# The first prompt tile's output projection moved from the merge block to the end of the sample attention's block

## Chip, cores and metric

The kernel runs on one core of a Trainium2 chip (trn2), in float32. The metric is the device time of one execution in microseconds (us). "Runs" below are executions without the profiler; a profile is one further execution that the hardware profiler recorded.

## What is computed

One layer of a decoder for 512 prompt tokens and 64 sample tokens (8 sequences of 8), width 1024. Cut to what matters here:

```
x = x_prompt (512 rows), x_sample (64 rows)
sh1, sc1, ga1, sh2, sc2, ga2 = split(silu(c) @ w_ada + b_ada)
h   = rms_norm(x, g_pre_mix) * (1 + sc1) + sh1
z   = h @ w_in                                  # q, k, v, u, s
a   = rms_norm(attend(q, k, v), g_subln)        # prompt: causal; sample: 2048 cached keys + its own
s   = gelu(u) * (spatial gating of layer_norm(gelu(zs)))
mix = concat([a, s], -1) @ w_out                # the projection of this change: 1024 x 1024
x   = x + ga1 * rms_norm(mix, g_post_mix)
h2  = rms_norm(x, g_pre_ffn) * (1 + sc2) + sh2
y   = top-1 of 4 groups, top-2 of 4 experts (SwiGLU) on h2
out = x + ga2 * rms_norm(y, g_post_ffn)
```

## The kernel before

The kernel is written engine by engine, with semaphores set by hand. An engine works through its own list in order; nothing is reordered by a scheduler. The program is a row of blocks: condition, project and `attend_prompt` in one; `attend_sample` in a block of its own; then `merge` and `experts`; then the rest. At a block's end each engine drains and all meet (line 930 for the sample block). After the sample block `forget` (from line 243) clears semaphores and has all engines meet once more. Then each jumps to its part of `merge`.

The 576 tokens are five tiles, t = 0 to 3 with 128 prompt tokens each and t = 4 with the 64 sample tokens. `attend_prompt` has written the prompt tiles' rows of `mix` before the sample block begins, so tile 0's projection needs nothing of the sample attention.

**The sample block's tail.** `values(f)` (lines 1172 and 1175) is the last TensorE work for a sequence. ScalarE copies half of its result (line 1011), VectorE adds, masks and reduces (1097, 1100, 1105), and GpSimd stores it (966), waits for the last two stores, and drains. SyncE has loaded `w_out` in two halves of 2 MB into ring slots 0 and 1 in this block (line 946).

**The merge block.** For tile t TensorE turns the rows of `mix` round with 8 transposes (`mix_tr`, line 1573), ScalarE and VectorE each copy half of them to `mixT` (`evac_mix`, 1323 and 1389), and TensorE runs 16 matmuls of 128x512 (line 1611; each has two rows in the trace, so a tile has 32). ScalarE squares the result and sums it (1359), GpSimd takes the power -1/2 (737, 738), VectorE scales it and adds x (1435, 1436: `x1_done`). ScalarE squares x1 (1365) and VectorE makes h2 (1441, 1442). While TensorE projects tile t it waits, before its second half, for `x1_done` of tile t-1.

What stands first on two engines matters here. ScalarE's list in `merge` begins with `evac_mix(0)`, and then issues 21 loads on its own queue: `g_post_mix`, `g_pre_ffn` and three rows of the modulation (these five raise `mod_in`), x of tile 0 among them (1336 to 1341), x of the other tiles (1343), eight pieces of the sample output (1345) and three more (1348). Then comes the loop over tiles, the square first. VectorE's part begins so:

```
dve.wait_ge(self.table_in, 64)
link(dve.memset(self.logits, 0.0))
evac_mix(0)
dve.wait_ge(mod_in, 16 * 5)
modulation(0, P)
for t in range(NT):
    ...
    if t + 1 < NT:
        evac_mix(t + 1)
```

`modulation` (lines 1408, 1409) multiplies the loaded rows. So VectorE's copy for tile 1 stands behind the wait for `mod_in`, and ScalarE's copy for tile 1 stands behind its loads and the square of tile 0. SyncE's expert weights (line 1211) wait for `mod_in` and all x.

Of the kernel before, what the change touches and what calls it, by code (L numbers as in the profile page):

```python
# [18 lines left out]
ACT = mybir.ActivationFunctionType  # L19
# [4 lines left out]
P = 128  # L24
D = 1024
KC = D // P
# [39 lines left out]
def rows(t):  # L66

    return P if t < 4 else NS
# [117 lines left out]
class Program:  # L186
    def __init__(self, nc, a, o, where, ncst, ctx):
# [17 lines left out]
        self.mod_outs = self.lasting("mod_outs")  # L205
        self.mod = nc.dram_tensor("mod_rows", (NS + 1, 6 * D), F32).ap()
# [697 lines left out]
    def attend_sample(self):  # L904
# [25 lines left out]
        with nc.Block() as block:  # L930
# [50 lines left out]
            def _(act):  # L981
# [34 lines left out]
                looped(act, step)  # L1016

            @block.vector
            def _(dve):
# [87 lines left out]
                looped(dve, step)  # L1107

# [95 lines left out]


# [9 lines left out]
    def merge(self, block):  # L1215
# [3 lines left out]
        (o_in, ss_ready, ss_power, mix_ready, mod_in, tr_done, ev_a, ev_d, proj_done, sq1, rs1, x1_done,  # L1219
# [3 lines left out]
                 "o_in", "ss_ready", "ss_power", "mix_ready", "mod_in", "tr", "ev_a", "ev_d", "proj",  # L1223
# [13 lines left out]
        mixT = [L.at(L.HT + D * i, D).rearrange("p (k t) -> p k t", k=KC) for i in range(2)]  # L1237
# [46 lines left out]
        def proj_bank(t, c):  # L1284

            return 3 if c == 1 - t % 2 else (4 if c else 2)
# [30 lines left out]
        def _(act):  # L1317
            def evac_mix(t):
                n = rows(t)
                act.wait_ge(tr_done, t + 1)  # L1320
                if t >= 2:
                    act.wait_ge(proj_done, t - 1)
                act.activation(mixT[t % 2][:, 0:4, 0:n],
                               PS[:, 0, :].rearrange("p (k t) -> p k t", k=4)[:, :, 0:n], ACT.Copy).then_inc(ev_a, 1)

# [8 lines left out]
            evac_mix(0)  # L1334
# [15 lines left out]
            for t in range(NT):  # L1350
                n = rows(t)
                if t < 4:
                    act.wait_ge(proj_done, t + 1)
                else:
                    act.wait_ge(summed, 2)
                if t >= 2:
                    act.wait_ge(h2_tr, t - 1)
                    act.wait_ge(h2_out2[t % 2], 16 * (t // 2))
                act.activation(hv[t % 2][0:n], proj(t, n), ACT.Square, accum_out=ss1[0:n, t:t + 1]).then_inc(sq1, 1)
                if t >= 1:  # L1360
                    evac_h2(t - 1)
                if t + 1 < NT:
                    evac_mix(t + 1)
                act.wait_ge(x1_done, t + 1)
                act.activation(hv[t % 2][0:n], self.x1[0:n, t, :], ACT.Square,
                               accum_out=ss2[0:n, t:t + 1]).then_inc(sq2, 1)
                act.wait_ge(h2_done, t + 1)
                act.dma_start(self.h2[P * t:P * t + n, :], hv[t % 2][0:n]).then_inc(h2_out2[t % 2], 16)
# [12 lines left out]
        def _(dve):  # L1381
            link = chain(dve, dchain)

            def evac_mix(t):
                n = rows(t)
                dve.wait_ge(tr_done, t + 1)
                if t >= 2:
                    dve.wait_ge(proj_done, t - 1)
                dve.tensor_copy(mixT[t % 2][:, 4:8, 0:n],  # L1389
                                PS[:, 1, :].rearrange("p (k t) -> p k t", k=4)[:, :, 0:n]).then_inc(ev_d, 1)  # L1390
# [22 lines left out]
            evac_mix(0)  # L1413
            dve.wait_ge(mod_in, 16 * 5)
            modulation(0, P)
            for t in range(NT):
# [13 lines left out]
                if t + 1 < NT:  # L1430
                    evac_mix(t + 1)
# [132 lines left out]
        def _(pe):  # L1564
            def mix_tr(t):
                n = rows(t)
                if t >= 1:
                    pe.wait_ge(ev_a, t)
                    pe.wait_ge(ev_d, t)
                if t == 4:  # L1570
                    pe.wait_ge(mix_ready, 1)
                for k in range(KC):
                    last = pe.transpose(PS[:, k // 4, (k % 4) * P:(k % 4) * P + n], L.mix[0:n, t, k::KC],
                                        L.cst("ident", n)[:, 0:n])
                last.then_inc(tr_done, 1)
# [22 lines left out]
            mix_tr(0)  # L1598
            for t in range(NT):
                n = rows(t)  # L1600
                pe.wait_ge(ev_a, t + 1)
                pe.wait_ge(ev_d, t + 1)
                for i, c in enumerate((t % 2, 1 - t % 2)):
                    if t == 0:
                        pe.wait_ge(self.ring_full[W_OUT[c]], 16 * STATIC_USES[W_OUT[c]] + 16)
                    if t >= 2 - i:
                        pe.wait_ge(x1_done, t - 1 + i)
                    w = L.ring[W_OUT[c]].rearrange("p (k n) -> p k n", k=KC)
                    if t < 4:
                        for k in range(KC):  # L1610
                            last = pe.matmul(PS[:, proj_bank(t, c), :], mixT[t % 2][:, k, :], w[:, k, :],  # L1611
                                             start=k == 0, stop=k == KC - 1)
# [9 lines left out]
                if t >= 1:  # L1622
                    h2_tr_of(t - 1)
                if t + 1 < NT:
                    mix_tr(t + 1)
                if t >= 1:
                    logits_of(t - 1)
# [440 lines left out]
```

## Time and profile before

| | before |
|---|---|
| median of 3 runs | 1033.86 us (1033.08 to 1035.77) |
| the profiled execution's own time | 1031.1 us |
| its span in the trace | 1029.3 us |
| mean granted TensorE clock, share of full | 0.907 |
| TensorE (PE) busy | 825.5 us, 80% of the span |
| VectorE (DVE) busy | 345.0 us, 34% |
| ScalarE (ACT) busy | 210.0 us, 20% |
| GpSimd (POOL) busy | 121.7 us, 12% |
| DMA | 257.52 MB, mean 250 GB/s |

The span is that of one execution; its own time is 1.8 us longer, and 2.8 us under the median of the runs. A share of busy time is a mean over stages with different limits, so what counts for this change is read from the stretch between 545 and 600 us, where the sample block ends and the merge begins.

### The profile page before, as it was taken

The numbers are of one execution on the slowest core, as the hardware profiler recorded it, in microseconds if no ns is written. First come the engines' busy times: TensorE is split into PE (matmuls) and PEld (weight loads), VectorE is DVE, ScalarE is ACT, GpSimd is POOL, SyncE is SP. The second block draws the span as 40 slices with busy tenths as digits, with TensorE's granted clock in tenths as the row PEclk, the third lists the DMA queues.
The fourth block names the chain that finished last, engine by engine and source line by source line (L and its number), as shares of the span: only waits on it lengthen the run. The fifth ranks groups of instructions, "written<-read, shape, count | busy, mean of one in ns | idle before, by whom it ended". The sixth has DMA issues, their size and how long they took to land. (4 is left out here: it accounts for less than half of the span.)

```text
span 1029.3 us, 12324 instructions
## 1 busy us (share of the span) xinstructions
PE 825.5 (80%) x4656; PEld 429.3 (42%) x4656; DVE 345.0 (34%) x799; ACT 210.0 (20%) x437; POOL 121.7 (12%) x204
## 2 busy tenths in 40 slices
PE   0329999999788869899875999249998999999940
PEld 0024444444455545665642455234443444444410
DVE  0143630021578755555530354530110111001017
ACT  0200100100556423433420121100110111111113
POOL 1310100000400011322210010010000000000024
PEclk9959999999679889999986999559999999999975
DMA  8959412382892017999972951514789899999835
GB/s 258 253 165 348 169 56 77 118 305 65 316 401 65 1 61 309 389 414 425 378 285 113 337 223 61 205 62 173 273 327 411 354 388 399 377 415 379 346 115 192
DMA packets 49293, 257.52 MB, mean 250 GB/s; under 512 B 5704, under 2 KB 6952, under 8 KB 38880
## 3 DMA queue, kind: packets, MB, share of 16 engines
q1 hardware_dynamic: 30224, 151.54, 38.7%
q0 software_dynamic: 10672, 86.72, 22.1%
q10 hardware_dynamic: 8352, 18.66, 5.7%
q8 instruction: 29, 0.48, 0.2%
q14 instruction: 16, 0.13, 0.0%
HBM read 234.07 MB, written 22.83 MB: 250 GB/s over the span
## 5 line engine op out<-in xcount | busy, mean ns | idle before, releaser
L695 PE MATMUL ps<-sb 128*128 128x512 f32 x320 | 142.8, 601 | 0.0
L1820 PE MATMUL ps<-sb 128*128 128x512 f32 (+1 forms) x256 | 114.2, 599 | 0.0
L695 PEld LDWEIGHTS ps<-sb 128*128 128x128 f32 x320 | 60.3, 192 | 73.7 <-issue 73.3
L1122 PE MATMUL ps<-sb 128*128 128x128 f32 x512 | 64.9, 281 | 18.4 <-ACT sb L991 9.3
L1774 DVE TENSOR_TENSOR sb<-sb,ps 128x512 f32<-128x512 f32 (+1 forms) x16 | 10.9, 684 | 190.9 <-PE ps L1820 127.6
L1122 PEld LDWEIGHTS ps<-sb 128*128 128x128 f32 x512 | 56.7, 143 | 31.7 <-issue 17.4
L1812 PE MATMUL ps<-sb 128*128 128x512 f32 x144 | 66.8, 618 | 1.0 <-ACT sb L1738 0.8
L1833 PE MATMUL ps<-sb 128*128 128x512 f32 x144 | 63.5, 594 | 0.0
L1611 PE MATMUL ps<-sb 128*128 128x512 f32 x128 | 58.8, 619 | 1.9 <-DVE sb L1389 0.9
L1817 PE MATMUL ps<-sb 128*64 128x512 f32 x112 | 50.9, 608 | 7.5 <-DMA sb<-in_w_up 7.5
L1820 PEld LDWEIGHTS ps<-sb 128*128 128x128 f32 (+1 forms) x256 | 42.5, 168 | 34.4 <-issue 34.4
L879 PE MATMUL ps<-sb 128*128 128x128 f32 (+3 forms) x128 | 53.2, 556 | 3.2 <-ACT sb L792 3.2
L442 PE MATMUL ps<-sb 128*9 128x512 f32 x192 | 22.6, 624 | 39.6 <-DMA sb<-in_w_ada 39.6
L1038 DVE COPY sb<-ps 128x512 f32<-128x512 f32 x64 | 41.2, 685 | 21.0 <-PE ps L1122 21.0
L805 ACT ACTIVATE sb<-sb 128x128 f32<-128x128 f32 (+3 forms) x64 | 35.4, 554 | 41.9 <-DVE sb L859 41.9
L1812 PEld LDWEIGHTS ps<-sb 128*128 128x128 f32 x144 | 27.7, 198 | 33.7 <-issue 31.8
L991 ACT ACTIVATE sb<-ps 128x512 f32<-128x512 f32 x64 | 34.8, 595 | 32.3 <-PE ps L1122 32.0
L1833 PEld LDWEIGHTS ps<-sb 128*128 128x128 f32 x144 | 26.7, 190 | 31.0 <-issue 30.9
L1611 PEld LDWEIGHTS ps<-sb 128*128 128x128 f32 x128 | 25.1, 199 | 32.9 <-issue 30.4
L1781 DVE COPY sb<-ps 128x512 f32<-128x512 f32 (+1 forms) x16 | 11.1, 692 | 77.6 <-PE ps L1833 54.5
L1172 PE MATMUL ps<-sb 128*32 128x256 f32 x512 | 32.2, 404 | 5.8 <-DMA sb<-in_cache_v,ints 4.7
L1135 PE MATMUL ps<-sb 128*32 128x512 f32 (+1 forms) x320 | 36.6, 530 | 0.0
(254 smaller groups left out, 984.2 us busy)
## 6 DMA issues: line engine op xcount, KB each, us to landing
sb<-in_w_gate SPq DMA_DIRECT2D x16, 2048.0 KB, 12.5
sb<-in_w_up SPq DMA_DIRECT2D x16, 2048.0 KB, 16.9
sb<-in_w_down SPq DMA_DIRECT2D x16, 2048.0 KB, 8.4
sb<-in_w_ada SPq DMA_DIRECT2D x12, 2048.0 KB, 12.8
sb<-in_w_in SPq DMA_DIRECT2D x5, 2048.0 KB, 16.6
y_rows<-sb POOLq DMA_DIRECT2D x1, 5120.0 KB, 36.8
y_rows<-sb SPq DMA_DIRECT2D x9, 512.0 KB, 8.8
sb<-in_x_prompt ACTq DMA_DIRECT2D x8, 512.0 KB, 11.9
```

Of the source, the lines that this page charges most:

```text
L695: last = pe.matmul(PS[:, n % 4, :], L.hT[:, k, t * P:t * P + P], w[:, k, :], start=k == 0, stop=k == KC - 1)
L805: act.activation(pb[n % 3][j][:, 0:w], pb[n % 3][j][:, 0:w], ACT.Exp, bias=nm[:, q:q + 1], accum_out=sums[:, q:q + 1]).then_inc(exp_done, 1)
L879: pe.matmul(PS[:, 2 * (n % 2) + j, 0:P * (i + 1)], qz[i % 2][:, h // 2, 2 * (h % 2) + j, :], L.kT[:, h // 2, 0:P * (i + 1)], start=True, s ...
L991: act.activation(kt[ch % 2][:, h, :], PS[:, h, :], ACT.Copy).then_inc(kt_act, 1)
L1038: dve.tensor_copy(kt[ch % 2][:, h, :], PS[:, h, :]).then_inc(kt_dve, 1)
L1122: last = pe.transpose(PS[:, h, P * g:P * g + P], kp[:, 4 * (ch % 2) + g, P * h:P * h + P], L.cst("ident"))
L1135: last = pe.matmul(bank[32 * h:32 * h + 32, 0:512 if ch < 4 else NS], qst[par][:, h, :], rhs, start=True, stop=True)
L1611: last = pe.matmul(PS[:, proj_bank(t, c), :], mixT[t % 2][:, k, :], w[:, k, :], start=k == 0, stop=k == KC - 1)
L1812: last = pe.matmul(PS[:, 0, :], x[:, k, :], w_gate[:, k, :], start=k == 0, stop=k == KC - 1)
L1817: last = pe.matmul(PS[n:P, 0, :], x[:, k, :], w_gate[:, k, :], start=k == 0, stop=k == KC - 1)
L1820: last = pe.matmul(PS[0:n, 1, :], x[:, k, :], w_up[:, k, :], start=k == 0, stop=k == KC - 1)
L1833: last = pe.matmul(PS[:, 5 + c, :], hT[:, k, :], w[:, k, 512 * c:512 * c + 512], start=k == 0, stop=k == FC - 1)
```

## The change

Tile 0's transposes, its two copies and its 16 matmuls are taken out of `merge` and put behind the last `values` of the sample block, on the same three engines. The bodies become methods of the program (`mix_transpose`, `mix_evac_act`, `mix_evac_dve`, `mix_half`), and four semaphores outlive the block. In `merge`, TensorE begins with tile 1's transposes. The banks, the buffers, the weights and the arithmetic stay the same. The method bodies that the diff removes from `merge` are cut here.

```diff
@@ -1014,6 +1016,7 @@
                         act.activation(S[par], S[par], ACT.Exp, bias=nm[:, par:par + 1],
                                        accum_out=sums[:, par:par + 1]).then_inc(exp_done, 1)
                 looped(act, step)
+                self.mix_evac_act(act, 0)
 
             @block.vector
             def _(dve):
@@ -1105,6 +1108,7 @@
                         dve.tensor_reduce(om[1 - par], osum.rearrange("p g d -> p d g"), AX, ALU.add
                                           ).then_inc(o_ready, 1)
                 looped(dve, step)
+                self.mix_evac_dve(dve, 0)
 
             @block.tensor
             def _(pe):
@@ -1202,6 +1206,60 @@
                         values(f)
                 looped(pe, step)
 
+                pe.wait_ge(kt_act, 2 * 4 * SB)
+                pe.wait_ge(kt_dve, 2 * 4 * SB)
+                self.mix_transpose(pe, 0)
+                pe.wait_ge(self.mix_ev_a, 1)
+                pe.wait_ge(self.mix_ev_d, 1)
+                for c in range(2):
+                    pe.wait_ge(self.ring_full[W_OUT[c]], 16 * STATIC_USES[W_OUT[c]] + 16)
+                    last = self.mix_half(pe, 0, c)
+                last.then_inc(self.proj_done, 1)
+
+
+    def mix_buffers(self):
+        L = self.L
+        return [L.at(L.HT + D * i, D).rearrange("p (k t) -> p k t", k=KC) for i in range(2)]
+
+    def mix_transpose(self, pe, t):
+
+        n = rows(t)
+        for k in range(KC):
+            last = pe.transpose(self.PS[:, k // 4, (k % 4) * P:(k % 4) * P + n], self.L.mix[0:n, t, k::KC],
+                                self.L.cst("ident", n)[:, 0:n])
+        last.then_inc(self.mix_tr, 1)
+
+    def mix_evac_act(self, act, t):
+
+        n = rows(t)
+        act.wait_ge(self.mix_tr, t + 1)
+        if t >= 2:
+            act.wait_ge(self.proj_done, t - 1)
+        act.activation(self.mix_buffers()[t % 2][:, 0:4, 0:n],
+                       self.PS[:, 0, :].rearrange("p (k t) -> p k t", k=4)[:, :, 0:n], ACT.Copy
+                       ).then_inc(self.mix_ev_a, 1)
+
+    def mix_evac_dve(self, dve, t):
+
+        n = rows(t)
+        dve.wait_ge(self.mix_tr, t + 1)
+        if t >= 2:
+            dve.wait_ge(self.proj_done, t - 1)
+        dve.tensor_copy(self.mix_buffers()[t % 2][:, 4:8, 0:n],
+                        self.PS[:, 1, :].rearrange("p (k t) -> p k t", k=4)[:, :, 0:n]).then_inc(self.mix_ev_d, 1)
+
+    def proj_bank(self, t, c):
+
+        return 3 if c == 1 - t % 2 else (4 if c else 2)
+
+    def mix_half(self, pe, t, c):
+
+
+        w = self.L.ring[W_OUT[c]].rearrange("p (k n) -> p k n", k=KC)
+        for k in range(KC):
+            last = pe.matmul(self.PS[:, self.proj_bank(t, c), :], self.mix_buffers()[t % 2][:, k, :], w[:, k, :],
+                             start=k == 0, stop=k == KC - 1)
+        return last
 
     def load_expert(self, sp, e, par, kind):
 
@@ -1331,7 +1380,6 @@
                 act.activation(h2T[t % 2][:, 0:4, 0:m],
                                PS[:, 5, :].rearrange("p (k t) -> p k t", k=4)[:, :, 0:m], ACT.Copy).then_inc(h2_ev, 1)
 
-            evac_mix(0)
             row_of = lambda c: self.mod[NS, c * D:(c + 1) * D].partition_broadcast(P)
             act.dma_start(g_post, a["g_post_mix"].partition_broadcast(P)).then_inc(mod_in, 16)
             act.dma_start(mod[0], row_of(2)).then_inc(mod_in, 16)
@@ -1410,7 +1450,6 @@
 
             dve.wait_ge(self.table_in, 64)
             link(dve.memset(self.logits, 0.0))
-            evac_mix(0)
             dve.wait_ge(mod_in, 16 * 5)
             modulation(0, P)
             for t in range(NT):
@@ -1428,7 +1467,7 @@
                 if t >= 1:
                     evac_h2(t - 1)
                 if t + 1 < NT:
-                    evac_mix(t + 1)
+                    self.mix_evac_dve(dve, t + 1)
                 dve.wait_ge(rs1, t + 1)
                 dve.wait_ge(x_in[t], 16)
 
@@ -1563,16 +1602,11 @@
         @block.tensor
         def _(pe):
             def mix_tr(t):
-                n = rows(t)
-                if t >= 1:
-                    pe.wait_ge(ev_a, t)
-                    pe.wait_ge(ev_d, t)
+                pe.wait_ge(ev_a, t)
+                pe.wait_ge(ev_d, t)
                 if t == 4:
                     pe.wait_ge(mix_ready, 1)
-                for k in range(KC):
-                    last = pe.transpose(PS[:, k // 4, (k % 4) * P:(k % 4) * P + n], L.mix[0:n, t, k::KC],
-                                        L.cst("ident", n)[:, 0:n])
-                last.then_inc(tr_done, 1)
+                self.mix_transpose(pe, t)
 
             def h2_tr_of(t):
                 n = rows(t)
@@ -1595,23 +1629,18 @@
                                          self.w_r[:, k, :], start=k == 0, stop=k == KC - 1)
                 last.then_inc(log_done, 1)
 
-            mix_tr(0)
-            for t in range(NT):
-                n = rows(t)
+            mix_tr(1)
+            for t in range(1, NT):
                 pe.wait_ge(ev_a, t + 1)
                 pe.wait_ge(ev_d, t + 1)
                 for i, c in enumerate((t % 2, 1 - t % 2)):
-                    if t == 0:
-                        pe.wait_ge(self.ring_full[W_OUT[c]], 16 * STATIC_USES[W_OUT[c]] + 16)
                     if t >= 2 - i:
                         pe.wait_ge(x1_done, t - 1 + i)
-                    w = L.ring[W_OUT[c]].rearrange("p (k n) -> p k n", k=KC)
                     if t < 4:
-                        for k in range(KC):
-                            last = pe.matmul(PS[:, proj_bank(t, c), :], mixT[t % 2][:, k, :], w[:, k, :],
-                                             start=k == 0, stop=k == KC - 1)
+                        last = self.mix_half(pe, t, c)
                     else:
 
+                        w = L.ring[W_OUT[c]].rearrange("p (k n) -> p k n", k=KC)
                         for k in range(KC // 2):
                             for c0, kk in ((0, k), (NS, k + KC // 2)):
                                 last = pe.matmul(PS[c0:c0 + NS, proj_bank(t, c), :], mixT[t % 2][:, kk, 0:NS],
```

What this makes of the engines' lists is below. "x16" counts instructions alike in a row; the line numbers are those of each program (1228, 1238, 1248 and 1260 are the new methods' lines, in the order transposes, ScalarE's copy, VectorE's copy, matmuls).

TensorE around the end of the sample block (the two branches are the block's end and the jump to `merge`), before:

```order
L1172 MATMUL ps<-sb 32x256 x32
L1175 MATMUL ps<-sb 32x256 x2
L930 UNCONDITIONAL_BRANCH
L1563 UNCONDITIONAL_BRANCH
L1573 MATMUL ps<-sb 128x128 x8
L1611 MATMUL ps<-sb 128x512 x16
L1573 MATMUL ps<-sb 128x128 x8
L1611 MATMUL ps<-sb 128x512 x16
L1584 MATMUL ps<-sb 128x128 x8
```

The same place with the change:

```order
L1176 MATMUL ps<-sb 32x256 x32
L1179 MATMUL ps<-sb 32x256 x2
L1228 MATMUL ps<-sb 128x128 x8
L1260 MATMUL ps<-sb 128x512 x16
L932 UNCONDITIONAL_BRANCH
L1602 UNCONDITIONAL_BRANCH
L1228 MATMUL ps<-sb 128x128 x8
L1260 MATMUL ps<-sb 128x512 x16
L1618 MATMUL ps<-sb 128x128 x8
```

One group of 8 transposes and 16 matmuls has moved ahead of the two branches; tile 1's group is now the first of the merge.

VectorE at the same place, from the last reduction of the sample output to tile 0's x1, before:

```order
L1105 TENSOR_REDUCE sb<-sb 64x64
L930 UNCONDITIONAL_BRANCH
L1380 UNCONDITIONAL_BRANCH
L1412 MEMSET sb 128x100
L1389 COPY sb<-ps 128x512
L1408 TENSOR_TENSOR sb<-sb 128x1024
L1409 SCALAR_TENSOR_TENSOR sb<-sb 128x1024
L1389 COPY sb<-ps 128x512
L1435 SCALAR_TENSOR_TENSOR sb<-ps,sb 128x1024
```

With the change:

```order
L1108 TENSOR_REDUCE sb<-sb 64x64
L1248 COPY sb<-ps 128x512
L932 UNCONDITIONAL_BRANCH
L1428 UNCONDITIONAL_BRANCH
L1452 MEMSET sb 128x100
L1448 TENSOR_TENSOR sb<-sb 128x1024
L1449 SCALAR_TENSOR_TENSOR sb<-sb 128x1024
L1248 COPY sb<-ps 128x512
L1474 SCALAR_TENSOR_TENSOR sb<-ps,sb 128x1024
```

Tile 0's copy has moved ahead of the branches; tile 1's copy still stands behind the two operations of `modulation`.

ScalarE from its jump into the merge to tile 1's copy, with the change (before, tile 0's copy, `L1323 ACTIVATE`, stood between the branch and the first load):

```order
L1373 UNCONDITIONAL_BRANCH
L1384 DMA sb<-in_g_post_mix 128x1024
L1385 DMA sb<-mod_rows 128x1024
L1386 DMA sb<-in_x_prompt 128x1024
L1387 DMA sb<-in_g_pre_ffn 128x1024
L1388 DMA sb<-mod_rows 128x1024
L1389 DMA sb<-mod_rows 128x1024
L1391 DMA sb<-in_x_prompt 128x1024 x3
L1391 DMA sb<-in_x_sample 64x1024
L1393 DMA sb<-o_sample 8x8x64 x8
L1396 DMA sb<-mod_rows 64x1024 x3
L1407 ACTIVATE sb<-ps 128x1024
```

The loads are now the first thing in the merge's list; the square of tile 0 (line 1407) and tile 1's copy stand behind all of them, as they did.

## Rows read from the trace of the kernel before

**Rows 1.** The page's first part: busy time (share of the span) and instructions.

```profile
PE   825.5 (80%) x4656; PEld 429.3 (42%) x4656; DVE 345.0 (34%) x799; ACT 210.0 (20%) x437; POOL 121.7 (12%) x204
```

**Rows 2.** Timeline, TensorE, 545 to 600 us: start, duration, work [idle before <-releaser].

```profile
546.91 3.04 PE L1172 MATMUL ps<-sb 128*32 128x256 f32 x32 [2.31 <-DMA sb<-in_cache_v,ints]
549.87 1.07 PE L1175 MATMUL ps<-sb 64*32 64x256 f32 x4
559.54 1.94 PE L1573 MATMUL ps<-sb 128*128 128x128 f32 x8 [8.60 <-PEq L243]
562.38 16.79 PE L1611 MATMUL ps<-sb 128*128 128x512 f32 x32 [0.91 <-ACT sb L1323]
579.01 1.04 PE L1573 MATMUL ps<-sb 128*128 128x128 f32 x8
581.00 13.97 PE L1611 MATMUL ps<-sb 128*128 128x512 f32 x32 [0.95 <-DVE sb L1389]
```

**Rows 3.** One line's instructions, 930 (block end), then 243: count, duration ns, start.

```profile
L930 PEldq DRAIN  x1: 3448/3448/3448, 547.5 to 547.5; - x1
L930 POOLq DRAIN  x1: 2832/2832/2832, 555.4 to 555.4; - x1
L243 PEldq EVENT_SEMAPHORE  x1: 51/51/51, 559.4 to 559.4; - x1
```

**Rows 4.** Timeline, VectorE, from 552 to 583 us.

```profile
552.30 0.58 DVE L1105 TENSOR_REDUCE sb<-sb 64x64 f32<-64x256 f32 x1
561.59 0.69 DVE L1389 COPY sb<-ps 128x512 f32<-128x512 f32 x1 [1.86 <-PE ps L1573]
...
573.40 1.23 DVE L1408 TENSOR_TENSOR sb<-sb 128x1024 f32<-128x1024 f32 x1 [11.11 <-DMA sb<-mod_rows]
574.54 1.22 DVE L1409 SCALAR_TENSOR_TENSOR sb<-sb 128x1024 f32<-128x1024 f32 x1
...
581.30 1.28 DVE L1435 SCALAR_TENSOR_TENSOR sb<-ps,sb 128x1024 f32<-128x1024 f32 x1 [0.45 <-POOL sb L738]
582.62 1.23 DVE L1436 TENSOR_TENSOR sb<-sb 128x1024 f32<-128x1024 f32 x1
```

**Rows 5.** Timeline, ScalarE and its queue (ACTq), from 561 to 581 us.

```profile
561.52 0.35 ACTq L1336 DMA_DIRECT2D sb<-in_g_post_mix  x1
...
573.21 1.77 ACTq L1348 DMA_DIRECT2D sb<-mod_rows  x3
579.21 1.02 ACT L1359 ACTIVATE sb<-ps 128x1024 f32<-128x1024 f32 x1 [17.10 <-PE ps L1611]
580.22 0.59 ACT L1323 ACTIVATE sb<-ps 128x512 f32<-128x512 f32 x1
```

**Rows 6.** Windows: stretch, its length, busy (x count) of each engine, PEclk, DMA share, GB/s.

```profile
551.00:554.00 3.00, 0.00 (x0) 0.00 (x0) 1.41 (x3) 0.37 (x1) 0.53 (x1) 1.00 0.00 0
562.30:566.00 3.70, 3.62 (x5) 1.58 (x6) 0.00 (x0) 0.00 (x0) 0.00 (x0) 0.50 0.76 249
566.00:570.00 4.00, 4.00 (x9) 1.70 (x7) 0.00 (x0) 0.00 (x0) 0.00 (x0) 0.74 0.98 353
586.00:600.00 14.00, 14.00 (x73) 8.09 (x72) 6.36 (x7) 2.24 (x5) 0.74 (x2) 1.00 1.01 427
373.90:377.00 3.10, 3.10 (x15) 3.10 (x16) 1.62 (x5) 1.19 (x2) 0.00 (x0) 0.51 0.66 198
```

**Rows 7.** Timeline, SyncE's queue (SPq), and TensorE's first work for an expert.

```profile
501.77 1.32 SPq L946 DMA_DIRECT2D sb<-in_w_out  x2
...
640.63 0.33 SPq L1211 DMA_DIRECT2D sb<-in_w_up  x1
...
686.00 1.97 PE L1795 MATMUL ps<-sb 128*128 128x128 f32 x8 [5.79 <-DMA sb<-h_rows,ints]
```

More of the change, by code:

```diff
@@ L205, in __init__ @@
         self.mod_outs = self.lasting("mod_outs")
+        self.mix_tr, self.mix_ev_a, self.mix_ev_d, self.proj_done = (
+            self.lasting(n) for n in ("mix_tr", "mix_ev_a", "mix_ev_d", "mix_proj"))
         self.mod = nc.dram_tensor("mod_rows", (NS + 1, 6 * D), F32).ap()
@@ L1218, in merge @@
         nc, a, L, PS = self.nc, self.a, self.L, self.PS
-        (o_in, ss_ready, ss_power, mix_ready, mod_in, tr_done, ev_a, ev_d, proj_done, sq1, rs1, x1_done,
+        tr_done, ev_a, ev_d, proj_done = self.mix_tr, self.mix_ev_a, self.mix_ev_d, self.proj_done
+        (o_in, ss_ready, ss_power, mix_ready, mod_in, sq1, rs1, x1_done,
          sq2, rs2, h2_done, h2_tr, h2_ev, log_done, log_read, h2_out, exp_in, exp_out, hot_done, rank_done,
@@ L1222, in merge @@
              self.sem("e_" + n) for n in (
-                 "o_in", "ss_ready", "ss_power", "mix_ready", "mod_in", "tr", "ev_a", "ev_d", "proj",
+                 "o_in", "ss_ready", "ss_power", "mix_ready", "mod_in",
                  "sq1", "rs1", "x1", "sq2", "rs2", "h2", "h2_tr", "h2_ev", "log", "log_read", "h2_out",
@@ L1236, in merge @@
         osb = L.at(L.V + 2048, 512, 0, NS)
-        mixT = [L.at(L.HT + D * i, D).rearrange("p (k t) -> p k t", k=KC) for i in range(2)]
+        mixT = self.mix_buffers()
         h2T = [L.at(L.HT + 2048 + D * i, D).rearrange("p (k t) -> p k t", k=KC) for i in range(2)]
@@ L1282, in merge @@
         table_made = self.sem("e_table_made")
-        def proj_bank(t, c):
-            return 3 if c == 1 - t % 2 else (4 if c else 2)
+        proj_bank = self.proj_bank
         def proj(t, n):
@@ L1317, in _ @@
         def _(act):
-            def evac_mix(t):
-                n = rows(t)
[L1320 to L1324, printed above, removed]
             def evac_h2(t):
@@ L1362, in _ @@
                 if t + 1 < NT:
-                    evac_mix(t + 1)
+                    self.mix_evac_act(act, t + 1)
                 act.wait_ge(x1_done, t + 1)
@@ L1382, in _ @@
             link = chain(dve, dchain)
-            def evac_mix(t):
-                n = rows(t)
[L1386 to L1390, printed above, removed]
             def evac_h2(t):
@@ L1430, in _ @@
                 if t + 1 < NT:
-                    evac_mix(t + 1)
+                    self.mix_evac_dve(dve, t + 1)
                 dve.wait_ge(rs1, t + 1)
@@ L1565, in mix_tr @@
             def mix_tr(t):
-                n = rows(t)
-                if t >= 1:
-                    pe.wait_ge(ev_a, t)
-                    pe.wait_ge(ev_d, t)
+                pe.wait_ge(ev_a, t)
+                pe.wait_ge(ev_d, t)
                 if t == 4:
                     pe.wait_ge(mix_ready, 1)
-                for k in range(KC):
-                    last = pe.transpose(PS[:, k // 4, (k % 4) * P:(k % 4) * P + n], L.mix[0:n, t, k::KC],
-                                        L.cst("ident", n)[:, 0:n])
-                last.then_inc(tr_done, 1)
+                self.mix_transpose(pe, t)
             def h2_tr_of(t):
@@ L1596, in logits_of @@
                 last.then_inc(log_done, 1)
-            mix_tr(0)
-            for t in range(NT):
-                n = rows(t)
+            mix_tr(1)
+            for t in range(1, NT):
                 pe.wait_ge(ev_a, t + 1)
@@ L1621, in _ @@
                     last.then_inc(proj_done, 1)
-                if t >= 1:
-                    h2_tr_of(t - 1)
+                h2_tr_of(t - 1)
                 if t + 1 < NT:
                     mix_tr(t + 1)
-                if t >= 1:
-                    logits_of(t - 1)
+                logits_of(t - 1)
             h2_tr_of(NT - 1)
```

## The prediction

> **What bounds the kernel now.** I read the page first: TensorE (PE) is busy for 80% of the span [rows 1], so an idle stretch of TensorE is where a gain would have to come from. Then I read the timeline of TensorE between 545 and 600 us. The last pass of the sample attention ends at 549.87 + 1.07 = 550.94, and tile 0's transposes begin at 559.54 after 8.60 us idle [rows 2]. From there TensorE works almost without pause: tile 0's matmuls from 562.38 to 579.17, tile 1's from 581.00 to 594.97 [rows 2]. The reader should see two things there: the pause of 8.6 us before tile 0, and that the pauses after it are under 1 us.
>
> What fills the 8.6 us is seen in the rows of the block's end. GpSimd's drain begins at 555.4 and takes 2832 ns, so it ends at 558.25; TensorE's own drain had ended with its last pass (547.5 + 3.448 = 550.95) [rows 3]. The second meeting of the engines ends with TensorE's semaphore event at 559.4, and the merge is entered at about 559.5 [rows 2, 3]. So from the last drain to the entry it takes 559.5 - 558.25 = 1.3 us.
>
> Then I looked at what else the merge's opening must do. VectorE sits 11.11 us in a wait for the modulation rows and starts `modulation` at 573.40; its two operations end at 574.54 + 1.22 = 575.76 [rows 4]. ScalarE's first load is issued at 561.52, 2.0 us after the entry, because tile 0's copy stood ahead of it, and the last at 573.21 + 1.77 = 574.98 [rows 5]. Today all of this lies under tile 0's matmuls, which end later, at 579.17 [rows 2]. That is the fact on which the forecast rests: **tile 0's projection is at once the cover for the loads.** Moved into the block before, it no longer covers them, since the loads are only issued once the merge is entered.
>
> **The change part by part.** I write E for the entry of the merge before (559.5) and E' for the entry after.
>
> *Added at the end of the sample block.* 8 transposes, two copies, 16 matmuls. The first transpose can start when the last pass ends, 550.95. Before, the matmuls began 562.38 - 559.54 = 2.84 us after the transposes' start [rows 2]; after the change ScalarE is free, and VectorE is free at 552.30 + 0.58 = 552.88 [rows 4], just when the transposes would end (550.95 + 1.94 = 552.89). So the matmuls start at 553.8. `w_out` was asked for at 501.77 [rows 7], 52 us earlier, so its wait costs nothing; if that cover were gone, each late microsecond would count in full. The sample output's last reduction and its store are issued ahead of the new copy on VectorE and by GpSimd, so they are not delayed.
>
> *How long they take.* Tile 0 before took 16.79 us, tile 1 13.97 us, with the same 32 passes [rows 2]. The difference, 2.8 us, is the clock: the granted clock was 0.50 of full, which is 1.2 GHz, from 562.3 to 566, a mean of 0.74 from 566 to 570, and 1.00, which is 2.4 GHz, while tile 1 ran [rows 6]. After the change TensorE comes to this work with a pause of only 0.9 us behind it, and the window from 551 to 554 shows 1.00, though with TensorE idle in it [rows 6]. So the projection costs between 14.0 us (all at 2.4 GHz) and 16.8 us (as before). Neither row is nearer to the new case; I take the middle, 15.4. It ends at 553.8 + 15.4 = 569.2 (567.8 to 570.6).
>
> The Trainium skill has a rule on this (TensorE: Matmul & The Clock Gate, Part 1: The HAM clock gate): the lower clock is the resting state and activity lifts it. By that rule TensorE, which has worked with short pauses since 547, would run the whole projection at 2.4 GHz, and the sum below would be 1.4 us smaller, 5.8. The trace of tile 0 before, which ran for several microseconds at the lower clock after a long pause, does not decide this for a start without a long pause, so I do not lean on it.
>
> *The meeting at the block's end.* It now waits for TensorE instead of GpSimd, whose stores and drain (until 558.25) lie under the projection. E' = 569.2 + 1.3 = 570.5, so E' - E = 11.0 us (9.6 to 12.4). The work queued behind it is the whole merge on all engines, above all ScalarE's loads.
>
> *Removed from the merge.* The transposes, copies and matmuls of tile 0: 579.17 - 559.5 = 19.7 us of TensorE's path. What is late next is tile 1's start, and this is read from the two queues behind which its copies stand:
>
> - VectorE: before, from the first load's issue to the modulation rows took 573.40 - 561.52 = 11.9 us, and `modulation` was done at 14.2 [rows 4, 5]. The loads are the same ones in the same order, so I keep 14.2. Then its copy, 0.69 [rows 4]: 14.9 us after the first issue.
> - ScalarE: 574.98 - 561.52 = 13.5 us of issuing, then the square of tile 0 (its result has long been there), 580.22 - 579.21 = 1.0, and its copy, 0.59 [rows 5]: 15.1 to 15.2.
>
> Add 0.2 us from the copy's end to the matmuls (580.81 to 581.00 [rows 2, 5]) and 0.1 from the entry to the first issue. Tile 1's matmuls then start at E' + 15.5 = 586.0, against 581.00 before: **5.0 us later**. Tile 1's transposes need about 2 us after E' and lie far under this. On VectorE x1 of tile 0 follows the copy and comes about 2.6 us of work later (1435 and 1436, [rows 4]), well before tile 1's second half asks for it.
>
> *Tile 1 starts after a pause.* TensorE now stands still for some 13 us before it. Before, 8.6 us of pause were followed by slow matmuls. At another block's start, the stretch from 373.9 to 377 ran at 0.51 [rows 6], so about 3 us of work at half speed, which loses 1.5 us. Tile 0 before lost 2.8. The cost is thus 1.5 to 2.8, since a pause of this length has no row of a full-speed start; I take 2.2.
>
> *Everything later* hangs on tile 1's end: tiles 2 to 4, the routing, the expert weights asked for at 640.63 and the experts from 686.00, which wait for rows that the routing picked [rows 7]. Nothing there is tied to an absolute time, so the delay passes on whole. The four semaphores that outlive the block cost nothing I can see: their signals replace others on the same instructions.
>
> *Sum:* 11.0 - 21.5 (581.0 - 559.5) + 15.5 + 2.2 = **+7.2 us**. The bounds are 9.6 - 6.0 + 1.5 = +5.1 and 12.4 - 6.0 + 2.8 = +9.2. Against the profiled execution's own time, 1031.1 (span 1029.3), this gives 1038.3. The median of the runs lies 2.8 us above that execution, so on the median it is 1033.86 + 7.2 = 1041.1.
>
> **The rivals.**
>
> *Faster: the merge does not wait for TensorE's matmuls.* If the engines' meeting needed only TensorE's queue of instructions to be issued, not worked off, E' would stay at 559.5 while the projection runs on until 569.2. The loads would be issued 1.9 us earlier than before, tile 1 would start at 559.5 + 15.5 = 575.0 instead of 581.0, and with 0 to 2.8 us for the clock the gain is 3 to 6 us, so about 1029. It decides if the drain returns more than 3 us before the last matmul. Against it: TensorE's drain at the block's end took 3448 ns and ended just where the last pass did [rows 2, 3]. Chance 4%.
>
> *No change: the loads' queues do not hold tile 1.* If VectorE's and ScalarE's copies could run at once, tile 1's first half would start at E' + 2.8 and end by E' + 11. Its second half needs x1 of tile 0, which needs `modulation` (E' + 14.3) and the two operations of 2.6 us: E' + 16.9. With 7.0 to 8.4 us for the half (half of 14.0 or 16.8) it ends at E' + 23.9 to E' + 25.3, that is 594.4 to 595.8 against 594.97, so -0.6 to +0.8 us, about 1034. For it speaks only that the loads might land earlier now. Against it: the order of both lists, and ScalarE's 13.5 us of issuing, which by itself holds tile 1. Chance 6%.
>
> *Much slower: the clock stays low through the projection.* At half of full clock 32 passes would take twice 13.97 = 27.9 us instead of 15.4, so +19.7 in all, 1053.6. The window after 551 at 1.00, and that tile 0 before reached full speed on its way [rows 6], speak against it. Chance 3%.
>
> **How the numbers follow.** The forecast (slower by 5 to 9 us) has 87%, the rivals 4, 6 and 3. A change of 0.3% (3.1 us) is about what a measurement of this kernel can tell from none. Faster is 0.04, same 0.06, slower 0.90. The predicted time is 1041.1. The range takes the bounds 5.1 and 9.2, which give 1039.0 and 1043.1, and the spread of the runs before, 1.9 us above the median and 0.8 below; I widen the lower side a little more because the loads may land earlier than before: 1037.0 to 1045.0.
>
> **What would show each step.** The projection's matmuls stand between about 553.8 and 569; the entry of the merge at 570.5, with TensorE's drain the last; the first load 0.1 us behind it; `modulation` 11.9 us later; TensorE idle for 13 us before tile 1, which starts near 586 at the lower clock and ends near 602. TensorE's total idle time would not fall but rise. If tile 1 starts before 581, or the drain ends before the last matmul, the forecast is wrong.

## The result and the profile after

The changed kernel took 1039.60 us (median of 20 runs), against 1033.37 for 20 runs of the kernel before. The ratio is 1.0058, with a 95% interval of 1.0041 to 1.0074: slower by 6.0 us (4.2 to 7.6). The forecast was slower by 7.2.

The profiled execution took 1036.88 us, with a span of 1035.2, 5.8 us more in its own time than the one of before. Below is TensorE's timeline around the change (start, duration, work, idle before and its releaser), to be held against [rows 2].

```profile
547.91 1.07 PE L1179 MATMUL ps<-sb 64*32 64x256 f32 x4
548.90 1.50 PE L1228 MATMUL ps<-sb 128*128 128x128 f32 x8
551.62 13.97 PE L1260 MATMUL ps<-sb 128*128 128x512 f32 x32 [1.21 <-ACT sb L1238]
567.10 1.13 PE L1228 MATMUL ps<-sb 128*128 128x128 f32 x8 [1.51 <-PEq L245]
582.15 16.56 PE L1260 MATMUL ps<-sb 128*128 128x512 f32 x32 [13.92 <-ACT sb L1238]
598.54 1.05 PE L1618 MATMUL ps<-sb 128*128 128x128 f32 x8
```

The pause of 8.60 us before tile 0 is gone, as intended. In its place a pause of 13.92 us stands before tile 1, and tile 1's matmuls take 16.56 us instead of 13.97. The profiler names ScalarE's copy (L1238) as what ended the pause. "The entry" of the merge is from here on the start of TensorE's first matmul in it, here 567.10.

The block's end is next, by line: engine, count, duration in ns, start. It answers to [rows 3].

```profile
L932 POOLq DRAIN  x1: 2832/2832/2832, 553.4 to 553.4; - x1
L932 PEldq DRAIN  x1: 7915/7915/7915, 557.7 to 557.7; - x1
L932 PEldq EVENT_SEMAPHORE  x1: 51/51/51, 565.8 to 565.8; - x1
```

GpSimd's drain ended at 556.2, and TensorE's at 557.7 + 7.915 = 565.6, with the last matmul (551.62 + 13.97). All engines then went on; the meeting waits for TensorE. VectorE and ScalarE in the merge, against [rows 4, 5]:

```profile
578.89 1.23 DVE L1448 TENSOR_TENSOR sb<-sb 128x1024 f32<-128x1024 f32 x1 [11.78 <-DMA sb<-mod_rows]
580.03 1.22 DVE L1449 SCALAR_TENSOR_TENSOR sb<-sb 128x1024 f32<-128x1024 f32 x1
581.29 0.69 DVE L1248 COPY sb<-ps 128x512 f32<-128x512 f32 x1
```

```profile
566.88 0.36 ACTq L1384 DMA_DIRECT2D sb<-in_g_post_mix  x1
...
578.67 1.77 ACTq L1396 DMA_DIRECT2D sb<-mod_rows  x3
580.49 1.02 ACT L1407 ACTIVATE sb<-ps 128x1024 f32<-128x1024 f32 x1 [29.45 <-issue]
...
581.51 0.59 ACT L1238 ACTIVATE sb<-ps 128x512 f32<-128x512 f32 x1
```

VectorE's copy for tile 1 ends at 581.98 and ScalarE's at 582.10. Both stand behind the loads, one behind their landing and one behind their issue, and they are done within 0.1 us of each other. The clock is in the windows (columns as in [rows 6]):

```profile
552.00:566.00 14.00, 13.59 (x32) 5.70 (x30) 0.00 (x0) 0.00 (x0) 0.05 (x1) 1.00 0.00 1
567.00:582.00 15.00, 1.13 (x8) 0.97 (x8) 3.17 (x4) 1.51 (x3) 0.21 (x2) 0.61 0.96 327
582.00:586.00 4.00, 3.85 (x5) 1.79 (x6) 2.51 (x2) 0.93 (x2) 0.55 (x1) 0.50 1.14 156
```

Tile 0 ran wholly at 2.4 GHz (1.00); tile 1's first 4 us ran at 1.2 GHz (0.50).

**One measure for all kernels.** Executions differ by some microseconds in stretches that no edit here touches. So for each profile I take the time from the end of the last `values` pass (548.98 here) to the end of tile 1's matmuls (598.71). It is 44.0 us before and 49.7 with the change: +5.7. The last pass itself came 2.0 us earlier than in the profile before, and the rest of the program, from tile 1's end on, took 2.2 us longer. Of that rest, the part up to the first expert's matmuls took 91.0 us within 0.15 in all 13 profiles, so tile 1's delay is passed on whole to there; what differs lies behind it, in the experts and what follows, 342.2 to 347.9 us over the 13 profiles without a pattern by edit that I can see. The measure has one weakness: it holds the time of tile 0's projection, which took 1.7 us more in some profiles than in others (below).

### The profile page after: what moved, and what is told of

The parts are those of the page before. It is cut to its first block and busy times, and to the rows that moved or that the text cites. A ratio compares the mean times of both kernels' runs of the same rounds, so it can differ in the third digit from the quotient of the medians.

```text
span 1035.2 us, 12325 instructions
## 1 busy us (share of the span) xinstructions
PE 821.3 (79%) x4656; PEld 424.8 (41%) x4656; DVE 344.1 (33%) x799; ACT 210.1 (20%) x437; POOL 120.9 (12%) x204
## 5 line engine op out<-in xcount | busy, mean ns | idle before, releaser
L1260 PE MATMUL ps<-sb 128*128 128x512 f32 x128 | 58.5, 617 | 15.1 <-ACT sb L1238 15.1
L881 PE MATMUL ps<-sb 128*128 128x128 f32 (+3 forms) x128 | 48.0, 509 | 3.2 <-ACT sb L794 3.2
L1808 DVE COPY sb<-ps 128x512 f32<-128x512 f32 (+1 forms) x16 | 11.1, 692 | 77.5 <-PE ps L1860 54.4
## 6 DMA issues: line engine op xcount, KB each, us to landing
sb<-in_x_prompt ACTq DMA_DIRECT2D x8, 512.0 KB, 11.9
```

The source lines that it names most:

```text
L881: pe.matmul(PS[:, 2 * (n % 2) + j, 0:P * (i + 1)], qz[i % 2][:, h // 2, 2 * (h % 2) + j, :], L.kT[:, h // 2, 0:P * (i + 1)], start=True, s ...
L1260: last = pe.matmul(self.PS[:, self.proj_bank(t, c), :], self.mix_buffers()[t % 2][:, k, :], w[:, k, :], start=k == 0, stop=k == KC - 1)
```

## The experiments

My theory: tile 0's projection was the cover for the merge's loads. Moved ahead of the meeting, it delays the meeting and so the loads, which then stand bare before tile 1, on two engines' queues. The rivals: one queue alone holds tile 1; or any work put before the meeting costs its length, whatever the loads do. "From the profile" is the measure above less that of before; ratios are to the kernel before on the same chip, with 95% intervals.

| kernel | ratio (interval) | from the profile |
|---|---|---|
| the change | 1.0058 (1.0041 to 1.0074) | +5.7 us |
| VectorE's copy first | 1.0046 (1.0019 to 1.0072) | +5.7 |
| both copies first | 1.0031 (1.0000 to 1.0062) | +4.4 |
| TensorE kept busy, 13 matmuls | 1.0045 (1.0020 to 1.0070) | +7.1 |
| the same, 16 matmuls | 1.0024 (1.0002 to 1.0046) | +4.8 |
| before, loads early | 1.0035 (1.0011 to 1.0059) | +3.5 |
| before, six loads, after the store | 1.0007 (0.9985 to 1.0028) | -0.8 |
| change, loads early | 0.9975 (0.9951 to 0.9999) | -3.2 |
| and the rest issued by SyncE | 0.9929 (0.9902 to 0.9957) | -7.0 |
| and both copies first | 0.9897 (0.9872 to 0.9922) | -6.8 |
| and tile 1 made ready in the block | 0.9891 (0.9862 to 0.9919) | -9.4 |
| change, half the projection moved | 0.9976 (0.9953 to 0.9999) | -1.5 |

In three of these profiles (both copies first, and the two with extra matmuls) tile 0's projection took 15.6 to 15.7 us instead of 13.97. Without these 1.7 us they would stand at +2.7, +5.4 and +3.1, close to what their ratios give (+3.2, +4.6 and +2.5 us).

### Which queue holds tile 1

VectorE's copy for tile 1 ahead of its wait for the modulation rows:

```diff
             link(dve.memset(self.logits, 0.0))
+            self.mix_evac_dve(dve, 1)
             dve.wait_ge(mod_in, 16 * 5)
...
-                if t + 1 < NT:
+                if 1 <= t < NT - 1:
                     self.mix_evac_dve(dve, t + 1)
```

> The changed kernel, with VectorE's copy for tile 1 put ahead of its wait for the modulation rows. My theory: tile 1 is held by two queues, VectorE's behind the modulation (14.9 us after the merge's entry) and ScalarE's behind 13.5 us of issuing loads (15.1 us). With one of them freed nothing moves: tile 1's matmuls still start about 15 us after the entry, ratio to before 1.005 to 1.006. Rival: the wait for the modulation rows alone holds tile 1. Then its first half starts about 3 us after the entry and the time is that of before, ratio 0.999 to 1.001.

Tile 1 started 15.1 us after the merge's entry, as with the change (timeline of TensorE):

```profile
570.20 1.12 PE L1228 MATMUL ps<-sb 128*128 128x128 f32 x8 [1.51 <-PEq L245]
585.25 16.60 PE L1260 MATMUL ps<-sb 128*128 128x512 f32 x32 [13.92 <-ACT sb L1238]
```

VectorE's copy now ended at 572.1, 13 us before it was of use. So VectorE's queue alone did not hold tile 1. That ScalarE's alone held it is not excluded by this kernel. The changed kernel's rows speak against it: had ScalarE been free there, VectorE's copy would still have ended at 581.98, 0.1 us before ScalarE's. The next kernel frees ScalarE's as well:

```diff
             act.dma_start(mod[2], row_of(3)).then_inc(mod_in, 16)
+            self.mix_evac_act(act, 1)
```

> As the kernel before this one, and ScalarE's copy for tile 1 put behind its sixth load, ahead of the other 15 loads and the square of tile 0. My theory: tile 1's first half starts about 4 us after the entry; its second half waits for x1 of tile 0, which needs the modulation (14.3 us after the entry) and comes at about 18.3. It ends at 25 to 27 us after the entry, as late as before counted from the end of the sample attention: 0.8 us faster to 1 us slower, ratio 0.999 to 1.001. Rival: the loads are not what holds the merge's opening, and the loss of 6 us stays (1.0055).

```profile
566.21 1.13 PE L1228 MATMUL ps<-sb 128*128 128x128 f32 x8 [1.48 <-PEq L245]
569.90 8.83 PE L1260 MATMUL ps<-sb 128*128 128x512 f32 x16 [2.55 <-ACT sb L1238]
585.05 9.81 PE L1260 MATMUL ps<-sb 128*128 128x512 f32 x16 [6.32 <-DVE sb L1477]
```

The mechanism is as expected: tile 1's first half starts 3.7 us after the entry, and the second waits for x1 of tile 0 (VectorE, L1477) until 18.8 us after it. It won less than expected, 4.4 us over before by the profile (3.2 by the runs, 0 to 6.4) instead of about 0. Of this, 1.7 us are in tile 0's projection, which here took 15.67 us, and 1.4 to 2.8 in the second half, which took 9.81 us where I had allowed 7.0 to 8.4: the pause of 6.3 us brought the clock down again. The loads still hold the merge's opening, only one step later: VectorE's modulation starts 13.1 us after the entry, when the rows have landed, and ScalarE's square of tile 0, behind its loads, 13.4.

### What the clock costs

Extra matmuls, 13 of them in the first kernel and 16 in the second, whose result nobody reads:

```diff
             mix_tr(1)
+            for k in range(13):
+                pe.matmul(PS[:, 6, :], mixT[0][:, k % KC, :],
+                          L.ring[W_OUT[0]].rearrange("p (k n) -> p k n", k=KC)[:, k % KC, :], start=True, stop=True)
             for t in range(1, NT):
```

> The changed kernel, with 13 matmuls of 128x512 into a bank that nobody reads at that time, between tile 1's transposes and its projection. They add work that the result does not need. My theory: of the loss some 2.6 us are tile 1's matmuls at the lower clock after the pause of 14 us (16.56 instead of 13.97). The extra matmuls take about 13 us inside that pause and end before tile 1 may start, so it starts at the same time and takes 14.0: 2.6 us faster than the changed kernel, ratio to before 1.003. Rival: the longer tile 1 has another cause than the pause (the x1 wait in its second half, or the loads beside it), and the time stays at 1.0055.

The extra matmuls ended 3.4 us before tile 1 could start, and tile 1 still took 15.67 us. That is 0.9 us less than with the change, where 2.6 had been expected. Its start came 15.7 us after the entry, 0.7 later than with the change (the modulation rows landed 12.7 us after the first issue instead of 12.0), and tile 0's projection took 15.64 us, 1.7 more. So by the profile this kernel is even 1.4 us slower than the changed one, and its ratio of 1.0045 can't be told from 1.0058. The windows of this kernel show why tile 1 was still slowed:

```profile
581.00:583.30 2.30, 2.30 (x6) 0.76 (x4) 0.00 (x0) 0.00 (x0) 0.00 (x0) 1.00 1.04 424
583.30:586.70 3.40, 0.04 (x1) 0.00 (x0) 3.05 (x3) 1.60 (x3) 0.76 (x2) 1.00 1.09 300
586.70:589.00 2.30, 2.25 (x4) 1.01 (x5) 2.26 (x2) 0.00 (x0) 0.00 (x0) 0.79 1.22 146
589.00:592.00 3.00, 3.00 (x6) 1.24 (x5) 0.86 (x2) 1.15 (x2) 0.75 (x2) 0.60 0.87 170
```

The clock was full until tile 1 had begun, and was lowered during its first microseconds. So I closed the pause:

> The kernel that keeps TensorE busy, with 16 extra matmuls instead of 13, so that they end about 1 us before tile 1 may start instead of 3.4 us. They add work that the result does not need. My theory: what lowers the clock for tile 1 is the pause itself, also one of 3.4 us; with a pause of about 1 us tile 1 takes 14.0 us instead of 15.7. Rival: tile 1 is slow for another reason, such as the loads that still run beside it, and takes 15.5 us or more again.

```profile
567.21 13.90 PE L1634 MATMUL ps<-sb 128*128 128x512 f32 x32
581.27 13.99 PE L1260 MATMUL ps<-sb 128*128 128x512 f32 x32 [0.16 <-ACT sb L1238]
```

The pause is now 0.16 us, shorter than the 1 us that I had aimed at. Tile 1 took 13.99 us, beside the same loads. So its 16.56 us with the change are 2.6 us of lower clock, caused by the pause. In this kernel tile 0's projection took 15.67 us instead of 13.97, which hides 1.7 of the 2.6 in the sum.

### The loads as such

The kernel before, with its loads at the end of the sample block. `early_loads` issues the five loads of `mod_in` and the five of x, in the same order, with the modulation rows put in places that are free by then.

```diff
                 looped(act, step)
+                self.early_loads(act)
...
-            act.dma_start(g_post, a["g_post_mix"].partition_broadcast(P)).then_inc(mod_in, 16)
...
```

> The kernel before (tile 0's projection in the merge), with the five loads of gains and prompt modulation rows and the five of x issued at the end of the sample block, into places free by then. My theory: before the change those loads lie wholly under tile 0's projection, so bringing them forward wins nothing: VectorE's wait of 11 us goes, and the ratio is 0.999 to 1.001. Rival: VectorE's wait for them is on the path that sets the end already, and 2 us or more are won (0.998 or less).

It became slower, which neither theory had said. The block's end tells:

```profile
L932 POOLq DRAIN  x1: 2832/2832/2832, 558.9 to 558.9; - x1
```

The last store of the sample output was issued at 552.68, and GpSimd's drain began 6.2 us later. Before, it was issued at 553.47 and the drain began at 555.4 [rows 3], 1.9 us later. The ten loads were issued from 550.21 to 555.87, five of them ahead of the store. The entry of the merge came 12.9 us after the last pass instead of 8.6. The Trainium skill says that DMAs from SyncE's, ScalarE's and GpSimd's queues share the same 16 DMA engines and interleave (Trainium Kernel Development and Optimization, Key Constraints); this trace agrees, with 6.2 us against 1.9 for a store of 16 KB, while the DMA engines were busy 0.96 of that time against 0.04 before. To test that it was the store:

```diff
+                act.wait_ge(o_out[0], 16 * 4)
+                act.wait_ge(o_out[1], 16 * 4)
                 self.early_loads(act)
```

`early_loads` has six loads here; those of x of tiles 1 to 4 stay in the merge.

> The kernel before with early loads, but ScalarE issues only six of them (gains, three modulation rows, x of tile 0), and only once the last stores of the sample output have landed; x of the other tiles stays in the merge. My theory: early loads cost the kernel before 3.5 us because the last store shared the DMA with them and landed 4.3 us later, which put off GpSimd's drain and the meeting. With the store landed first, GpSimd's drain ends as before and ScalarE's issuing ends about 0.8 us after it: ratio 1.000 to 1.001. Rival: the loads cost by running into the merge or by ScalarE's issuing, not by the store, and 1.003 stays.

The ratio is 1.0007 and the loss is gone. GpSimd's drain began 1.9 us after the store's issue again, and the merge was entered 9.2 us after the last pass. Loads brought forward win nothing measurable in the kernel before: they had been covered. This kernel differs from the one before it in two things, the order and the number of early loads. Two later kernels, both with all ten loads early, part them:

```profile
L934 POOLq DRAIN  x1: 2832/2832/2832, 562.1 to 562.1; - x1
L934 POOLq DRAIN  x1: 2832/2832/2832, 554.5 to 554.5; - x1
```

In the first (the change with early loads) the store was issued at 555.18, after the first two of the loads, and the drain began 6.9 us later, hidden under tile 0's projection. In the second (tile 1 made ready in the block) it was issued at 552.60, 2.1 us ahead of the first load, and the drain began 1.9 us later. So it is the order and not the number.

### The change without the bare loads

The same `early_loads` in the changed kernel, behind ScalarE's copy of tile 0:

> The changed kernel, with the same ten loads issued at the end of the sample block, behind ScalarE's copy of tile 0. The eight loads of the sample output and three of sample modulation rows stay at the head of ScalarE's list in the merge. My theory: these 11 still take 8.0 us to issue, then the square (1.0) and the copy (0.6), so tile 1 starts 9.7 us after the entry instead of 15.2, still at the lower clock: 5.4 us less than the changed kernel, about equal to before, ratio 0.999 to 1.002. Rival: the landing of the rows alone holds tile 1 and not ScalarE's queue, and it starts at 3.4 us and at full clock: ratio 0.992.

Tile 1 started 7.1 us after the entry, not 9.7, at the lower clock (15.68 us):

```profile
570.56 3.74 ACTq L1407 DMA_DIRECT2D sb<-o_sample  x8
574.33 1.77 ACTq L1410 DMA_DIRECT2D sb<-mod_rows  x3
576.15 1.02 ACT L1421 ACTIVATE sb<-ps 128x1024 f32<-128x1024 f32 x1 [21.21 <-issue]
```

The eight loads of the sample output took 3.74 us to issue instead of 5.87 before the change, where they came directly behind the other ten loads. ScalarE's queue still held tile 1: VectorE's copy had ended at 573.9. Then those 11 loads went from ScalarE's list to SyncE's (the lines added are shown):

```diff
+            for b in range(SB):
+                sp.dma_start(osb[ST * b:ST * b + ST].rearrange("t (h d) -> t h d", h=H),
+                              self.o_sample[b].rearrange("(h t) d -> t h d", h=H)).then_inc(o_in, 16)
+            for i, c in enumerate((2, 4, 3)):
+                sp.dma_start(mod[3 + i][0:NS], self.mod[0:NS, c * D:(c + 1) * D]).then_inc(mod_in_s, 16)
             sp.wait_ge(mod_in, 16 * 5)
```

> As the kernel before this one, with the 11 loads issued by SyncE instead of ScalarE. My theory: tile 1's matmuls start 3.4 us after the entry (modulation 2.4, VectorE's copy 0.7), with no long pause before them, so at full clock: 11.7 + 2.6 us less than the changed kernel, 8.6 less than before, ratio 0.992. Now the projection in TensorE's idle tail is a gain, since the cover that it took away is not needed. Rival: the move itself costs (a longer block, a later meeting of the engines), and no more than the 6 us of loss come back (1.000).

```profile
573.00 1.13 PE L1231 MATMUL ps<-sb 128*128 128x128 f32 x8 [1.51 <-PEq L247]
576.29 15.62 PE L1263 MATMUL ps<-sb 128*128 128x512 f32 x32 [2.16 <-DVE sb L1251]
```

Tile 1 starts 3.3 us after the entry (3.4 expected). It is still slowed by the clock after two short pauses, so 7.0 us are won by the profile and not 8.6. The move into TensorE's idle tail is a gain once nothing needs its cover; the rival, that the longer block costs by itself and the ratio stays at 1.000 or above, is refuted. Then both copies first:

> The kernel with early loads and SyncE's issuing, and in addition both copies for tile 1 put first in the merge, ahead of the modulation and of the square of tile 0. My theory: tile 1's matmuls start 2.1 to 2.8 us after the entry, 0.6 to 1.3 us earlier than there; its second half asks for x1 of tile 0 some 7 us later, when it is there. 9.2 to 9.9 us less than before, ratio 0.991. Rival: x1 of tile 0 now comes too late for the second half, and nothing more is won than without it (0.992).

And tile 1 made ready in the sample block (its transposes and copies ahead of tile 0's matmuls; of the edit, TensorE's line):

```diff
                 pe.wait_ge(self.mix_ev_a, 1)
                 pe.wait_ge(self.mix_ev_d, 1)
+                self.mix_transpose(pe, 1)
                 for c in range(2):
```

> The fastest so far (early loads, SyncE issuing, copies first), with tile 1's transposes and copies too put into the sample block, between tile 0's copies and its matmuls. My theory: tile 1's matmuls start right at the entry instead of 2.1 us after it, against 1.1 us more of transposes ahead of tile 0's matmuls: 1.0 us less, and up to 3 us less if the shorter pause (1.5 us) leaves the clock up; ratio 0.987 to 0.989. Rival: tile 1's second half now waits for x1 of tile 0, and nothing is won (0.990 to 0.991).

The first won nothing by the profile over the kernel before it (-6.8 against -7.0), since tile 1, which started 2.1 us after the entry, took 17.04 us. Its runs say more: their median is 1025.50 us against 1028.16 for the kernel before it on the same chip, and the ratio of 0.9897 (-10.7 us) is at least as good as the 0.991 expected. The profiled execution, 1028.61 us, was the slowest of its six. So most executions may have had the full clock in tile 1; no profile shows it, and the intervals of the two kernels overlap. The second is the fastest by the profile; its ratio, 0.9891, is not told apart from 0.9897:

```profile
554.49 14.73 PE L1266 MATMUL ps<-sb 128*128 128x512 f32 x32
570.71 13.97 PE L1266 MATMUL ps<-sb 128*128 128x512 f32 x32 [1.48 <-PEq L247]
```

One pause of 1.48 us is all that is left, and tile 1 took 13.97 us. It takes 1022.71 us (ratio 0.9891, 0.9862 to 0.9919), faster than both the kernel before and the changed one.

### Half of the projection

```diff
-                for c in range(2):
-                    pe.wait_ge(self.ring_full[W_OUT[c]], 16 * STATIC_USES[W_OUT[c]] + 16)
-                    last = self.mix_half(pe, 0, c)
-                last.then_inc(self.proj_done, 1)
+                pe.wait_ge(self.ring_full[W_OUT[0]], 16 * STATIC_USES[W_OUT[0]] + 16)
+                self.mix_half(pe, 0, 0)
...
+            pe.wait_ge(self.ring_full[W_OUT[1]], 16 * STATIC_USES[W_OUT[1]] + 16)
+            self.mix_half(pe, 0, 1).then_inc(proj_done, 1)
             mix_tr(1)
```

> The changed kernel, with only the first of tile 0's two halves (8 matmuls) in the sample block and the second in the merge. My theory: the block ends with TensorE 9.7 us after the last values, entry at 11.0 (8.6 before, 18.1 changed); the loads then run under the second half; tile 1 is still held 15.2 us after the entry, so at 26.2 against 30.1 before, and loses up to 2.6 us to the clock: 1.3 us faster than before (4 if the clock holds), ratio 0.996 to 0.999. Rival: work moved behind the meeting costs in proportion to what is moved, and half of the loss stays (1.003).

```profile
558.57 7.11 PE L1258 MATMUL ps<-sb 128*128 128x512 f32 x16 [1.56 <-ACT sb L1236]
566.98 7.10 PE L1258 MATMUL ps<-sb 128*128 128x512 f32 x16 [1.30 <-PEq L245]
582.58 15.85 PE L1258 MATMUL ps<-sb 128*128 128x512 f32 x32 [7.62 <-DVE sb L1246]
```

The entry came 11.1 us after the last pass (8.6 before) and tile 1 15.6 us later: 1.5 us faster by the profile, 1.3 forecast. Half of the work in the tail is a small gain where the whole is a loss: what the tail can hide is worth moving, what goes beyond it puts off the loads.

## Why the prediction was right

It held in direction, in cause and in size, and the steps can be checked one by one, counted from the end of the last pass (550.94 before, 548.98 after).

- *Start of the projection:* forecast 2.9 us after it, measured 2.6. The transposes took 1.50 us instead of the 1.94 assumed. VectorE's reduction ended 0.5 us after them (550.92 against 550.40), so VectorE's copy, done at 551.51, was the last thing waited for, not ScalarE's as the profiler's row has it. `w_out` cost nothing.
- *Its length:* taken as 15.4 between 14.0 and 16.8; measured 13.97 in this profile. This is the term that was mis-sized, by 1.4 us in this profile. The rule of the Trainium skill (TensorE: Matmul & The Clock Gate, Part 1) that I had set beside it, and not used, gave 14.0 and so 5.8 for the sum, which is nearer to the 5.7 measured. It does not hold every time, though: of nine profiles with all of tile 0's projection in the block, five show 13.97, one 14.73 and three 15.6 to 15.7, a mean of 14.6. In the four where the transposes ahead of it took 1.50 to 1.72 us, so that the clock rose only during them, it took 13.97. Of the five where they took 1.16 us, with the clock already full, one did, behind a pause of 1.55 us; in the three slow ones the granted clock fell to 0.50 behind a pause of 1.55 us. The profiled execution of the change was 2.7 us under the median of its runs, so others of its runs may have been slow here; this is not shown.
- *The meeting:* 1.3 us from the last drain to the entry forecast, 1.5 measured (565.6 to 567.1). TensorE's drain ends with the last matmul, so the rival by which the meeting does not wait for it is refuted.
- *Tile 1's start:* 15.5 us after the entry forecast, 15.1 measured. The modulation rows landed 12.0 us after the first issue (11.9 forecast), and ScalarE's issuing took 13.6 (13.5).
- *The clock in tile 1:* 2.2 forecast between 1.5 and 2.8; 2.6 measured, and shown to come from the pause by the kernel with 16 extra matmuls.
- *What comes later:* the forecast had the delay pass on whole. From tile 1's end to the first expert's matmuls it took 91.0 us before and 91.1 after.
- *The sum:* 18.1 - 8.6 = 9.5 later entry, less 21.5, plus 15.1, plus 2.6 is 5.7. The bounds 5.1 to 9.2 held it, and the forecast of 7.2 is 1.5 too high, nearly all of it from the projection's length. The other terms were off by 0.2 to 0.5 us each, in both directions.

The rival "no change" rested on x1 of tile 0 as the next wait. The kernel with both copies first shows that this wait is real (18.8 us after the entry; 16.9 and 18.3 expected). Of the 1.9 us above 16.9, 1.1 are the modulation, done 15.4 us after the entry instead of 14.3, and 0.8 the wait for tile 0's square and power on ScalarE and GpSimd, which the 16.9 had left out. By its profile that kernel came out 4.4 us slower and not level, as the clock was lowered twice, in tile 0's projection and in tile 1's second half. What stays open is when the clock falls after pauses of 1 to 4 us: one pause of 1.48 us before tile 1 left it at 13.97 us, while 1.51 and 2.16 us with the transposes between them were followed by 15.62, and 1.48 and 0.95 us by 17.04.

## What to carry to other kernels

Work that fills one engine's idle time may at the same time be the cover for loads, so before moving it ahead of a meeting of the engines, ask what was issued beside it and whether that can move too. Move into a tail only as much as the tail hides, or take the loads along, and then look at which engine's list the loads stand on: freeing one of the two queues gave nothing here. A change of this sort should be tried with its companion, since here the same move was worth +6 us alone and, with the loads early and off ScalarE, -7 to -11.

## What the runs showed of the hardware

- A 16 KB store let its engine go on 6.2 to 7.2 us after its issue (four profiles) when it was issued among ten loads of 0.25 to 0.5 MB, and 1.9 us after it when it was issued 2.1 us ahead of them, or without them.
- The same eight small loads took ScalarE 4.85 to 6.27 us to issue directly behind the other ten (seven profiles), and 3.02 to 3.74 where six or all of those had been issued at least 5 us earlier (three profiles).
- A pause of 3.4 us in TensorE's work cost 1.7 us in the matmuls after it, although the granted clock was still full when they began; it was lowered in their first microseconds.
- The same 32 float32 passes, behind pauses of 0.99 to 1.55 us, took from 13.97 to 15.67 us in eight profiles of the same code path.
